# Key and value projections of the second attention, interleaved instead of all keys first

## The reference, cut to what matters

```python
c_kv = rms_norm(ckv_full[..., :MLA_KV_LORA], ckv_norm)
kv = (c_kv @ w_ukv).reshape(b, s, MLA_HEADS, MLA_QK_NOPE + MLA_V_DIM)
k_nope = rms_norm(kv[..., :MLA_QK_NOPE], k_nope_norm)
v = kv[..., MLA_QK_NOPE:]
```

## Time and profile before

| what | value |
|---|---|
| median of 3 runs | 1310.92 us (1309.97 to 1312.26) |
| the profiled execution's own time | 1310.21 us |
| its span | 1308.4 us |
| granted TensorE clock, mean | 0.997 |
| busy share of PE, DVE, ACT, POOL | 96%, 67%, 53%, 28% |
| start of unit 8, first load of its weights | 471.30 us |
| start of the attention's third block of scores | 504.65 us |

### The profile page before, as it was taken

How to read it: one execution, slowest core, us unless ns; L and a number is a source line. 1 busy time by engine, 2 the same in 40 slices (tenths; PEclk the granted TensorE clock), 3 DMA queues, 4 the chain that set the end, 5 groups by cost and what they waited for, 6 DMA issues and landing times.

```text
span 1308.4 us, 24267 instructions
## 1 busy us (share of the span) xinstructions
PE 1258.7 (96%) x8884; PEld 1089.6 (83%) x8884; DVE 881.1 (67%) x1388; ACT 693.1 (53%) x1249; POOL 366.6 (28%) x377
## 2 busy tenths in 40 slices
PE   6999999999999999999999999999999999999996
PEld 5887899999998877898999998888855699987666
DVE  7868588666768985558976667853277548453774
ACT  5555455444567777535554547644377515413672
POOL 4952145344321140144344342011012320000022
PEclk9999999999999999999999999999999999999998
DMA  8565247566545533155666653422200364422100
GB/s 308 183 235 182 76 138 270 196 239 240 196 143 177 163 128 97 58 189 166 234 221 227 227 207 129 133 93 97 87 11 2 71 171 143 164 97 81 49 1 33
DMA packets 50505, 191.72 MB, mean 147 GB/s; under 512 B 5936, under 2 KB 6320, under 8 KB 48112
## 3 DMA queue, kind: packets, MB, share of 16 engines
q1 hardware_dynamic: 43632, 158.59, 36.4%
q0 software_dynamic: 6064, 31.33, 6.8%
q10 hardware_dynamic: 720, 0.57, 0.2%
HBM read 189.41 MB, written 1.05 MB: 146 GB/s over the span
## 4 chain that ended last, share of the span: by engine, by line
PE 80%; DVE 10%; ACT 6%; issue 2%; POOL 1%; DMA 1%; DVEq 0%; SPq 0%; ACTq 0%; POOLq 0%
PE G L428 14%; PE G L430 14%; PE G L429 14%; PE A L428 6%; PE A L430 6%; PE A L429 6%; DVE WL L1147 3%; PE R L655 2%; PE R L574 2%; PE G L1024 2%; ACT WH L1844 2%; PE R L428 1%; PE R L430 1%; PE R L429 1%; PE R L562 1%
## 5 line engine op out<-in xcount | busy, mean ns | idle before, releaser
L1147 DVE TENSOR_TENSOR WL<-RAW,WH 128x1024 fp32r<-128x1024 f32 x295 | 381.3, 1299 | 289.1 <-ACT WH L1844 288.7
L1844 ACT ACTIVATE WH<-RAW 128x1024 fp32r<-128x1024 f32 x295 | 310.4, 1057 | 412.0 <-PE G L430 302.6
L428 PE MATMUL G<-XH,WH 128*128 128x256 f32 (+1 forms) x1336 | 400.1, 299 | 9.7 <-DVE WL L1147 6.4
L429 PE MATMUL G<-XL,WH 128*128 128x256 f32 (+1 forms) x1336 | 394.9, 296 | 0.0
L430 PE MATMUL G<-XH,WL 128*128 128x256 f32 (+1 forms) x1336 | 394.9, 296 | 0.0
L428 PEld LDWEIGHTS G<-XH,WH 128*128 128x128 f32 x1336 | 255.3, 191 | 33.2 <-issue 25.8
L429 PEld LDWEIGHTS G<-XL,WH 128*128 128x128 f32 x1336 | 255.5, 191 | 6.3
L430 PEld LDWEIGHTS G<-XH,WL 128*128 128x128 f32 x1336 | 255.5, 191 | 6.3
L428 PE MATMUL A<-HH,WH 128*128 128x256 f32 x352 | 99.8, 283 | 3.7 <-POOL HL L2466 3.7
L429 PE MATMUL A<-HL,WH 128*128 128x256 f32 x352 | 99.6, 283 | 0.0
L430 PE MATMUL A<-HH,WL 128*128 128x256 f32 x352 | 99.5, 283 | 0.0
(11 more groups left out here) (347 smaller groups left out, 2354.5 us busy)
## 6 DMA issues: line engine op xcount, KB each, us to landing
RAW<-in_wst SPq DMA_DIRECT2D x295, 512.0 KB, 3.4
M<-in_wmod POOLq DMA_DIRECT2D x16, 1024.0 KB, 6.2
M<-in_wmod POOLq DMA_DIRECT2D x16, 512.0 KB, 6.4
B<-in_rpb POOLq DMA_DIRECT2D x4, 1024.0 KB, 11.3
H<-in_x_t SPq DMA_DIRECT2D x2, 512.0 KB, 7.7
M<-in_x_tok SPq DMA_DIRECT2D x1, 1024.0 KB, 11.6
M<-in_ctx_t POOLq DMA_DIRECT2D x1, 1024.0 KB, 5.1
out_y<-M SPq DMA_DIRECT2D x2, 384.0 KB, 2.7
```

The source lines that it names most:

```text
L428: mm(out, lh, rh, start=start, stop=False, skip_group_check=True)
L429: mm(out, lh, rl, start=False, stop=False, skip_group_check=True)
L1147: v.tensor_tensor(WL[:, slot, :], RAW[:, raw, :], WH[:, slot, :].bitcast(F32), ALU.subtract).then_inc(w_lo, 1)
L1844: act(WH[:, slot, :], RAW[:, raw, :], ACT.Copy).then_inc(w_hi, 1)
```

## The change

The eight units are reordered, and the host lays the eight panels in the same new order. Nothing else is edited; sizes, counts and bank rules stay.

```diff
-         + [(name, g, 2, 1) for name in ("ukn", "ukv") for g in range(4)])
+         + [(name, g, 2, 1) for name, g in (("ukn", 0), ("ukv", 0), ("ukn", 1), ("ukv", 1), ("ukn", 2), ("ukn", 3), ("ukv", 2), ("ukv", 3))])
...
+    kv = {name: _value_tiles(ukv[:, :, 128 * i:128 * i + 128].reshape(256, 2048), 4) for i, name in enumerate(("ukn", "ukv"))}
...
-        "l1_kv": np.concatenate([_value_tiles(ukv[:, :, 128 * i:128 * i + 128].reshape(256, 2048), 4) for i in range(2)]),
+        "l1_kv": np.concatenate([kv[name][8 * g:8 * g + 8] for name, g, kt, _ in TOKEN if kt == 2]),
```

## The result

The changed kernel is slower by a little: 1313.11 us median of 14 runs (1311.54 to 1315.73) against 1311.70 of 14 runs of the kernel before, a ratio of 1.0017 with a 95% interval of 1.0010 to 1.0024, that is 2.2 us (1.3 to 3.1). The means are 1313.27 and 1311.45, 1.8 apart. The profiled execution took 1311.79 with a span of 1310.0.

What follows compares the result with a forecast made beforehand. Two nearly full engines, TensorE and ScalarE, bound the stretch. Waits of 1.0 + 0.5 + 0.3 + 2.55 = 4.35 against 3.30 + 0.33 = 3.63 gave 0.7 us slower: 1310.92 + 0.7 = 1311.6 us, range 1309.2 to 1313.5.

Steps and rivals of the forecast that it cites:

- What bounds the kernel now: Units 8 to third scores: TensorE and ScalarE nearly full; TensorE waits 3.30 us at turns, leads the exponentials by 0.33.
- The waits that go: TensorE's waits at the key units' turns, 3.30 us in the old order, shrink to 1.0, 0.5 and 0.3.
- the walk: New order followed unit by unit with the old profile's distances: 0.7 us slower, between 0.2 and 1.5; chance 0.62.
- The wait that comes: In front of the first scores, TensorE waits 2.55 us for ScalarE's copy of the last keys; none before.
- The table load as before: ScalarE's table load ahead of the exponentials comes at 499.6 us, against 499.72 in the kernel before.
- The sum: All TensorE waits in the changed stretch: 4.35 us against 3.63 before, so 0.7 us slower.
- the clock rival: Behind the scores' wait TensorE drops to half clock: 2.0 us more, 2.7 slower in all, 1313.6 us; chance 0.07.
- The sign that I gave: In the changed kernel's profile, the granted clock column for the stretch stays at 1.00.
- Within 0.2%: Whole kernel's time differs from the kernel before by less than 0.2%, 2.6 us; chance 0.81.
- The low end of the bounds: With a scores' wait of only 1.3 us, exponentials set the third scores again and the time changes by 0.
- The other rivals: Whole kernel: stall goes, none comes, 1308.2 us (0.07); nothing changes, 1310.9 (0.14); turns wait as now, 1313.1 (0.10).

Runs made afterwards that it cites:

- the timed repeat: The changed kernel unaltered, run again on another chip beside the kernel before: ratio 1.0014, mean 1312.80 us.
- the keys' copy first: The changed kernel with ScalarE copying the last keys ahead of the two value copies in unit 14: ratio 1.0001 to the kernel before, mean 1311.05 us.
- the first experiment: Keys earlier: the kernel before with another mixed order, k0 k1 v0 k2 k3 v1 v2 v3 (k keys, v values): ratio 1.0002, mean 1311.29 us.
- the filled wait: The changed kernel with five extra 128x256 matmuls of constants on TensorE before the scores' wait: ratio 1.0005 to the kernel before, mean 1312.05 us.
- the delay in the old order: The kernel before with nine extra transposes on TensorE in front of the first scores: ratio 1.0012 to the kernel before.
- the version that should beat both: Order k0 k1 v0 k2 k3 v1 v2 v3, with unit 14's split and remainder moved behind the first exponentials: ratio 1.0000 to the kernel before, mean 1311.27 us.

## Why the prediction was right in its walk and wrong in its result, point by point

- **What bounds the kernel now** held. TensorE, ScalarE and VectorE are all nearly full in the stretch, and TensorE was only 0.33 us ahead of the exponentials at the third scores.
- **The waits that go.** I had 1.0, 0.5 and 0.3. The profile's first and second halves of each turn wait 0.78 and 0.39, 0.28 and 0.39, 0.26 and 0.28. By the starts of the units, which is how I had counted, the first is 486.06 - 481.40 - 3.63 = 1.03 and the second 492.86 - 486.06 - 6.27 (two units and a turn) = 0.53, and the third turn starts at 495.72 + 0.37 = 496.1, as in the walk. Right in size and place.
- **The wait that comes.** Forecast 2.55 for line 2184, measured 2.52 in the first profile, and 2.51 or 2.52 in the others of the changed kernel. That ScalarE's value copies stand in front of it was shown by moving them: 1.55 and no loss.
- **The table load as before**, at 499.6: measured 499.7.
- **The sum**, 0.7: measured 0.76 in the first profile, 0.7 to 0.8 in the three others whose clock stays high there.
- **The step that failed is the chance of the clock rival.** I wrote that the wait of 2.55 could be followed by the lower level, priced it at 2.0 us, and gave it 0.07 as a case that either holds for the kernel or doesn't. The runs show that it holds for a share of the executions, three of the seven profiled, at 1.5 to 1.6 us each. The expected cost is then 0.76 + 3/7 x 1.5 = 1.4, an estimate from these rows. The means say 1.8 and 1.9, with intervals (1.3 to 3.1, and 0.7 to 3.0 for the second) that hold it; the 0.4 to 0.5 us between is not shown to come from this place. I took the row at 373.26, where 1.84 us of waiting is followed by fast matmuls, as evidence that a wait of that length is safe. It was one execution: at this very place five of 14 profiles have the low clock. And I judged by the first matmul behind the wait, where in the first profile of the changed kernel the slow ones begin 1.5 us behind it. The sign that I gave, a clock column that stays at 1.00, held in the first profile's scores (499 to 512 us) and failed in the timed repeat, 0.87.
- **"Within 0.2%"** held for the measured ratio, 1.0017, though its interval reaches 1.0024. It missed what the interval shows: the sign is clear, slower, and the size is two to three times the 0.7.
- **The low end of the bounds**, that exponentials set the time again if the keys' copy comes soon enough, was shown by the keys' copy first: wait 0.36 for line 1899, ratio 1.0001.
- The other rivals fell. TensorE's gain at the turns did not shorten the chain of ScalarE and VectorE: the roots stand behind the squares still, and in the first experiment the saved time came back as a wait of 1.10 at the third scores.

Open: the filled wait speaks for the clock as the rest of the loss, but its interval touches the changed kernel's. A rival for a part of that rest is that the shift itself, without any wait in front of the scores, makes the low clock more frequent elsewhere, near 796 us for one. The mean clock of each run on record speaks for it. In the profiles a mean clock of 0.995 or less comes with two or three low stretches ahead of the program's last microseconds (three profiles of four that have so many, none of the ten others). Without the two runs at 0.946, such a mean clock stands in one of 59 executions of the kernel before, in none of 22 of the two kernels whose third scores come on time (keys earlier, keys' copy first), but in 11 of 30 of the changed kernel, in three of 11 of the delay in the old order, and in five of 11 of the version that should beat both, which comes 0.76 us early. The last two have no wait in front of the scores. Where their low stretches lie is not shown, and neither is how the other 1.0 us divides between the two places and causes.

## What to carry to other kernels

A reordering that removes waits in the middle of a stage is worth only what is left at the first point where its results are all needed: walk to that point, and look at what stands ahead of the last producer's copy on its queue. Interleave the heavy and the light units early, and leave the light ones for the end, so that the last heavy result has cover; here two value units or a swap of two copies did that. Neither made the kernel faster than the old order, because the chain of ScalarE and VectorE then set the time again. And price such a wait of TensorE at more than its own length: here the lower clock followed the one of 2.52 us in three of seven profiles, 1.5 us each time.

## What the runs showed of the hardware

The same program with the same wait has a low granted clock behind it in one execution and not in the next. Behind 1.85 us (two places) it was 10 of 28, behind 2.52 us 3 of 7, behind 4.03 us one profile and, by their times, probably most of eight runs. Each such stretch costs about 1.5 us where it stands, of which up to 0.4 is made up in the 100 us behind it, and the spread of the runs of the kernel before (1309.74 to 1313.16 in 35) is of the size of none, one or two of them. A difference under 2 us between two kernels has to be read from the rows, at places that both share, and not from two profiles' spans. The Trainium skill's page "TensorE: Matmul & The Clock Gate", section "What's actually happening", says that where a transition falls varies because what the gate watches runs free of the kernel's start. The traces agree in that the low stretch begins anywhere from 0.1 to 1.6 us behind the end of the wait of 1.85 us; they show besides that at one place it may not come at all.

Two engines also change each other's times. At about 552 us VectorE's remainder of 128x1024 took 1.23 us and GpSimd's sum of 128x512 about 2.1 where VectorE had started first (four profiles), and 1.74 to 1.89 us and 1.03 where GpSimd had (ten profiles), and all behind it came 0.4 us later in the ten.
